# A hybrid decoder layer on one core: one of three weight-block sums of the first down sweep moved from VectorE to an adding load on GpSimd's queue

## The reference

```
P   = RMSNorm(x) @ W_in           gated recurrence y_A and sparse attention y_B from its columns
x   = x + RMSNorm(concat(y_A, y_B) @ W_o)
h   = RMSNorm(x)
ff  = silu(h @ W_gate) * (h @ W_up)          hidden width 2816
out = x + RMSNorm(ff @ W_down)
```

## Time and profile before

| what | value |
|---|---|
| median of 3 runs | 664.42 us (663.7 to 664.64) |
| the profiled execution, its own time | 664.04 us |
| its span, first to last instruction | 662.3 us |
| VectorE busy | 541.6 us, 82% of the span |
| ScalarE busy | 346.5 us, 52% |
| GpSimd busy | 92.0 us, 14% |
| mean transfer rate | 114 GB/s |

### The profile page before, as it was taken

The page is one execution under the profiler, slowest core; times in us unless marked ns, Lnnn a source line. Parts: engine busy times, 40 slices in busy tenths (PEclk is TensorE's granted clock), DMA queues, the critical chain, the costliest instruction groups (busy, mean ns, idle before and its releaser), DMA issues.

```text
span 662.3 us, 10177 instructions
## 1 busy us (share of the span) xinstructions
PE 652.5 (99%) x4023; PEld 582.1 (88%) x4023; DVE 541.6 (82%) x756; ACT 346.5 (52%) x551; POOL 92.0 (14%) x131
## 2 busy tenths in 40 slices
PE   8999999999999999999999999999999999999996
PEld 6878888888888889888998999999999998788885
DVE  5766999998988768345987989989989879987876
ACT  5656433443349578334653554554555565664543
POOL 4800230000405379002100000000000000000001
PEclk9999999999999999999999999999999999999999
DMA  8443042343621300252342323234234226435433
GB/s 267 139 160 100 29 128 65 96 156 99 191 65 64 117 11 13 116 191 65 92 164 63 101 92 128 81 112 128 69 123 128 67 101 216 143 128 190 128 96 127
DMA packets 51106, 75.27 MB, mean 114 GB/s; under 512 B 5361, under 2 KB 40177, under 8 KB 50802
## 3 DMA queue, kind: packets, MB, share of 16 engines
q1 hardware_dynamic: 47200, 62.52, 29.8%
q0 software_dynamic: 3568, 11.55, 4.7%
q10 hardware_dynamic: 290, 0.55, 0.2%
HBM read 69.86 MB, written 6.84 MB: 116 GB/s over the span
## 4 chain that ended last, share of the span: by engine, by line
PE 89%; DVE 7%; ACT 2%; DMA 1%; issue 1%; POOL 0%; DVEq 0%; ACTq 0%; POOLq 0%
PE PS L1628 38%; PE PS L1968 27%; PE PS L2006 9%; PE PS L2017 3%; PE PS L1847 2%; PE PS L1702 2%; DVE W_r L1510 2%; PE PS L1678 1%; PE PS L1677 1%; PE PS L1858 1%; PE PS L1672 1%; PE PS L1781 1%; DMA A<-in_x_dram 1%; PE PS L1743 1%; PE PS L1712 1%
## 5 line engine op out<-in xcount | busy, mean ns | idle before, releaser
L1628 PE MATMUL PS<-hT_lo,w_hi 128*128 128x512 f32 (+2 forms) x280 | 102.0, 364 | 0.0
L1628 PE MATMUL PS<-hT_hi,w_hi 128*128 128x512 f32 (+2 forms) x280 | 100.7, 360 | 0.0
L1628 PE MATMUL PS<-hT_hi,w_lo 128*128 128x512 f32 (+2 forms) x280 | 100.6, 359 | 0.0
L1085 DVE TENSOR_TENSOR w_lo<-raw,w_hi 128x2048 fp32r<-128x2048 f32 x21 | 48.1, 2292 | 18.9 <-ACT w_hi L726 18.7
L1968 PE MATMUL PS<-hT_hi,W_r 128*128 128x256 f32 x216 | 61.1, 283 | 0.0
L1968 PE MATMUL PS<-hT_hi,s_w 128*128 128x256 f32 x216 | 61.1, 283 | 0.0
L1968 PE MATMUL PS<-hT_lo,s_w 128*128 128x256 f32 x216 | 61.1, 283 | 0.0
L1628 PEld LDWEIGHTS PS<-hT_hi,w_hi 128*128 128x128 f32 (+1 forms) x280 | 52.5, 188 | 8.5
L1628 PEld LDWEIGHTS PS<-hT_lo,w_hi 128*128 128x128 f32 (+1 forms) x280 | 52.6, 188 | 7.3 <-issue 0.2
L1628 PEld LDWEIGHTS PS<-hT_hi,w_lo 128*128 128x128 f32 (+1 forms) x280 | 52.6, 188 | 7.2
L1968 PE MATMUL PS<-s_t,s_w 128*128 128x256 f32 x288 | 57.8, 283 | 0.6 <-ACT PS L954 0.6
(11 more groups left out here) (304 smaller groups left out, 1692.6 us busy)
## 6 DMA issues: line engine op xcount, KB each, us to landing
raw<-in_w_in_dram SPq DMA_DIRECT2D x15, 1024.0 KB, 5.5
W_f<-in_w_gate_dram SPq DMA_DIRECT2D x9, 1024.0 KB, 5.3
W_f<-in_w_up_dram SPq DMA_DIRECT2D x9, 1024.0 KB, 5.3
W_f<-in_w_down_dram SPq DMA_DIRECT2D x18, 512.0 KB, 3.5
raw<-in_w_o_dram SPq DMA_DIRECT2D x4, 1024.0 KB, 5.0
W_f<-in_w_down_dram SPq DMA_DIRECT2D x9, 256.0 KB, 3.8
A<-in_x_dram SPq DMA_DIRECT2D x4, 512.0 KB, 6.5
A<-in_x_dram POOLq DMA_DIRECT2D x4, 512.0 KB, 5.8
```

Of the source, the lines that this page charges most:

```text
L1085: dve.tensor_tensor(lo, raw_view(j), hi.bitcast(F32), ALU.subtract).then_inc(s_lo, 1)
L1628: o = pe.matmul(out, lhs[a], rhs[b], start=(first and n == 0), stop=(last and n == 2))
```

## The change

In the first sweep, `step_sums` no longer makes q2 = y2 + x2. GpSimd waits for the step's own load and then issues a load of x2 (256 KB of `W_down`) that adds to q2 in the buffer. There are nine of these, one per step, each signalling one of four new semaphores, `s_dadd`. VectorE makes q1 = x1 + x2, then waits for `s_dadd`, then makes q3. GpSimd's wait for the last block results goes, and the load of the output gain now stands behind the nine adding loads on its queue.

```diff
+        s_dadd = [sem(f"down_first_sum_landed{i}") for i in range(4)]
...
             pool.dma_start(x2_d, A2[:, 0:TB * D]).then_inc(s_x2s, 16)
-            pool.wait_ge(s_gu2, 2 * NS)
+            for d in range(NB):
+                c = STEPS[d][1]
+                down_landed(pool, d)
+                pool.dma_start(step_raw(d)[:, D:D + 512], wd[2 * c * P:(2 * c + 1) * P, 512:D],
+                               accum_op=ALU.add).then_inc(s_dadd[d % 4], 16)
             pool.dma_start(gain_out, norm_post_ffn[0, :].partition_broadcast(P)).then_inc(s_go, 16)
...
                 if kind == "one":
-                    link(dve.tensor_tensor(q[:, 2], q[:, 2], q[:, 1], ALU.add))
-                    dve.tensor_tensor(q[:, 1], q[:, 0], q[:, 1], ALU.add)
+                    link(dve.tensor_tensor(q[:, 1], q[:, 0], q[:, 1], ALU.add))
+                    dve.wait_ge(s_dadd[d % 4], 16 * (d // 4 + 1))
                     dve.tensor_tensor(q[:, 3], q[:, 2], q[:, 0], ALU.add).then_inc(s_dsum, 1)
```

## The result

The changed kernel takes 680.64 us (median of 3 runs, 680.48 to 685.75) against 664.42: a ratio of 1.0273, 95% interval 1.0247 to 1.0299. That is slower, as forecast, but by 16.2 us where 4.9 were forecast, and above the range of 665.4 to 674.7. (The medians alone give 1.0244; the ratio is taken over all the runs, and the highest, 685.75, lifts it.) The profiled execution took 680.64, its span is 678.9.

What follows compares the result with a forecast made beforehand. TensorE was taken to bound the kernel, VectorE almost level. At L = 4.0, step 0 is 2.8 late, step 2 4.85, step 5 4.92, cumulatively; the change costs 4.9 us, giving 669.3 against the 664.42 median, range 665.4 to 674.7.

Steps and rivals of the forecast that it cites:

- the 0.39 us: TensorE's only wait for VectorE in the sweep, before step 5; all that a faster VectorE can give back.
- the chain load, adding load, sum, split: Each step's load, sum, split gains an adding load in series, which VectorE waits for ahead of the third sum.
- L: Time from GpSimd's issue of an adding load to its landing; taken as 4.0 us, plain-load bounds 2.4 and 5.3.
- L - 1.21: Lateness of step 0, because step 1's third sum starts later; 2.8 us at L = 4.0.
- The gain load: Moved from 549.67 behind step 8's add, roughly to 585 to 590; needed only at 654.39, so nothing waits.
- costs nothing beyond this: Add for step 0 is waited for while VectorE still waits for step 1's load, so it adds no delay.
- step 2: Starts 2L - 3.15 later, 4.85 us at L = 4.0, through the load and adding load of step 3.
- step 6: From step 5 on, the larger of 2L - 3.54 and 3L - 7.08 late, 4.92 us; the delay then stays.
- the two-step loop: A load issues only when the step four before is done; later steps repeat this loop and add nothing.
- The one that gave 680.7: Rival: adding load as slow as the 2 MB row, 7.8 us, step 5 16.3 late; chance 0.07.
- The quick load: Rival, third sums of steps 1 and 3: L under 2.43, so under 1.3 us slower; chance 0.12.
- The saving carried through: Rival: VectorE bounds the whole sweep, nine times 0.68 gives 6.2 us, 658.2; counted in the 0.03 for faster.

Runs made afterwards that it cites:

- experiment 1: Kernel before with the first of VectorE's three sums left out and no load in its place: 663.46 us, ratio 0.999.
- experiment 3: Kernel after, but VectorE makes all three sums and the adding loads of steps 1 to 8 go to a spare place nobody waits for: 664.59 us, ratio 1.0008.
- experiment 7: Kernel after, but VectorE makes all three sums of step 0; adding loads for steps 1 to 8 only: 679.65 us, ratio 1.0238.
- experiment 8: Kernel after with the adding load cut to 128 KB, VectorE adding the other half: 673.92 us, ratio 1.016.
- experiment 2: Kernel after with plain loads in place of the adding ones, so the sum is left out: 671.01 us, ratio 1.0107.
- experiment 6: Kernel after with SyncE loading the half that is added to first, on its own semaphore, and GpSimd waiting for that alone: 667.13 us, ratio 1.0058.
- experiment 11: Kernel after with SyncE holding back the load of step 4 until the adding load of step 3 has landed: 681.77 us, ratio 1.0269.
- Experiment 5: Kernel after with 41 useless matmuls put where TensorE waits for step 0: 680.16 us, ratio 1.0252.
- experiment 10: SyncE's changed load order and GpSimd's wait of experiment 6, adding loads at steps 4 and 6 alone, other steps as before: 664.65 us, ratio 1.0012.

## Why the prediction was wrong in size and right in direction

**What held.** That TensorE sets the end of the sweep and VectorE's saving is worth little: experiment 1, 0.7 us (0.1 to 1.3) where the 0.39 us stood. That the cost is the chain load, adding load, sum, split, and not the transfer: experiment 3. L = 4.0: 4.01 in the chain, for an adding load with hardly a load of SyncE beside it. That value was a choice between 2.4 and 5.3, and it came out right with some luck: no run shows that the second read is what makes the 1.2 us over a plain load. The formula L - 1.21 for step 0: with L = 3.78 it gives 2.57, and with GpSimd's start 0.3 us behind a landing rather than 0.13 it gives 2.7; experiment 7 measured 2.71. The gain load moved to 592.76 and nobody waited for it.

**What failed: the sum kept SyncE's loads at the 3.9 and 3.8 us, and L at one value, though the two now run at the same time.** I argued that a load of SyncE would be quicker, since the gain load was moved away from it, and that the add for step 0 "costs nothing beyond this". The added loads do to SyncE's what I had read from the gain load, and harder. Rows of before had shown that a load beside others is no 3.8 or 4.2: SyncE's 256 KB load issued at 553.93, beside that gain load, took 4.55. And of the four x loads on GpSimd's queue, issued 0.5 to 0.7 us behind one another, has the first, 4.2; the page of before has their median:

```profile
A<-in_x_dram POOLq DMA_DIRECT2D x4, 512.0 KB, 5.8
```

What follows is how late each place was along the chain, counting from a sweep that began 0.44 us earlier in this execution (step 0's load issued at 528.28 and 528.72):

| place | predicted late | measured late | the difference |
|---|---|---|---|
| step 0 | 2.8 | 549.24 + 0.44 - 544.58 = 5.1 | load of step 1 6.08 instead of 3.9, and GpSimd's start 0.3 us behind its landing instead of 0.13 |
| step 2 | 4.85 | 568.72 + 0.44 - 558.80 = 10.4 | the 2.3 of step 0; adding load of step 3 5.99 instead of 4.0; slow clock in step 0, 1.26 |
| step 6 | 4.9 | 596.24 + 0.44 - 581.35 = 15.3 | the 5.5 of step 2; load of step 7 4.81 instead of 3.8 and its adding load 6.13 instead of 4.0, 3.1 together; slow clock from step 2 on, 1.73 |
| end | 4.9 | 678.9 + 0.44 - 662.3 = 17.0 | the 10.4 of step 6; slow clock in step 6, 1.7 |

(The 1.26: the load of step 3, which waits for block results that TensorE makes inside step 0, left 555.69 - 549.24 = 6.45 us after the start of step 0, and 549.77 - 544.58 = 5.19 before. The 1.73: from the start of step 2 to that of step 4 it is 581.41 - 568.72 = 12.69 us, and it was 569.76 - 558.80 = 10.96. The 1.7: in the two traces the first matmul of step 6 is 596.24 - 581.35 = 14.89 us apart, the thirteenth 600.68 - 584.07 = 16.61, and from there the distance stays.) The collisions come to 2.3 + 2.0 + 3.1 = 7.4 us and the clock to 4.7; with the 4.9 forecast that is 17.0, the whole of it, in this one execution of each kernel. I carried the wait of step 2 through the sweep with no further loss; step 6 had such a loss because collisions stretched the two-step loop too.

**The term that was missing: TensorE's clock.** The kernel before never left it idle for more than 0.39 us in the sweep, so no row of the sweep before showed a price, and the sum has nothing for it. In the kernel after, the granted clock fell at the waits of 5.16, 3.84 and 2.80 us. The length of a wait alone does not decide it. Behind 2.30 and 1.88 us it fell (experiment 8: 0.66 over the next 5.0 us both times), and so it did behind 2.71 and 1.86 us (experiment 7); behind 2.32 and 2.15 (experiment 2), 2.16 (experiment 7), 1.81 (experiment 6) and 1.69 us (experiment 11) it stayed at 1.00. Experiment 5 shows for step 0 that the idle time is the cause.

**The rivals.** The one that gave 680.7 met the number by another way: it had an adding load of 7.8 us everywhere, and none took over 6.7. The quick load needed L under 2.43, and even the plain one takes 2.8. The saving carried through nowhere.

**The wider rule of the adding load.** Experiments 2 and 8 show that 256 KB cost 1.2 us more with the addition than without, and that 256 KB added take 1.0 to 1.1 us more than 128 KB. The Trainium skill (Collectives: The Full Stack, section The bandwidth ceiling: the fold count and why AG ≠ RS ≠ AR) says of the reducing step of a ReduceScatter in a ring of cores that it needs two reads where a copy needs one, and so runs at half the rate. The load here is no such step; the direction agrees with 4.0 us against 2.8, and these runs show no more than that.

**What stays open.** In the traces the collision depends on the starts. Where a load of SyncE started within some 0.5 us of a 256 KB adding load, the adding load took 5.6 to 6.7 us (kernel after, experiments 3, 5 and 7). Where it started 0.7 us or more behind it, the adding load kept to 3.6 to 4.2 and SyncE's load was the late one (6.08 us for step 1 in the kernel after). Where it had started 0.7 us or more ahead, the adding load took 4.5 to 5.4 in experiments 3 and 11, but 3.6 to 4.2 in experiment 6, beside its own step's load. Why it is so lopsided, and takes up to 2 us from either, no run takes apart. Nor does one tell why one wait of 2.3 us brings the lower clock and another does not. The mean busy share of the 16 DMA engines was 0.51 in 3.5 us of the adding load alone (experiment 11) and 0.80 in 4.3 us of the two together (kernel after, from 560.00), so they do share these engines.

## What to carry to other kernels

When two engines are level, price a moved operation by the chain it joins, and then price that chain's loads by rows in which another queue's loads run beside them; a row of an undisturbed transfer is the lower bound, not the value. A wait ahead of TensorE may cost more than itself, since the matmuls behind it can run at half the clock; here waits from 1.86 us up did so, though not all. And an adding load hurts least where its waiter has some 6 us to spare, or where it is issued before its neighbours start; even there it gained nothing here (experiments 6 and 10).

## What the runs showed of the hardware that was not expected

- GpSimd takes 865 ns to issue an adding load and 540 ns for the same load plain (0.55 was expected).
- A plain load of 256 KB on GpSimd's queue landed in 2.8 us undisturbed (up to 4.3 beside a load of SyncE), the adding one in 3.6 to 4.2 us undisturbed, and in up to 6.7 beside a load of SyncE.
- A load of 256 KB on SyncE's queue, 3.8 us before, took 6.1 us behind an adding load (kernel after, step 1).
- At steps 2 and 6 of the kernel after, TensorE first ran a few matmuls 0.23 to 0.34 us apart and only then at 0.43 us: the clock fell behind the end of the idle time. In experiment 7 it fell within it: the granted clock was 0.50 from 564.40 to 565.80, and step 2 started at 565.89.
